# Half of the second modulation's products set between the tiles of two projection groups, and the first modulation's steps in another order

## The chip, the cores and the metric

The kernel runs on one core of one Trainium2 chip. The metric is device time in microseconds (us) of one execution. Three timed runs of the kernel before gave 1221.15, 1223.98 and 1226.54 us; the median is 1223.98. Engines are named as the profile names them: PE is the matrix engine (PEld its weight load), ACT the scalar engine, DVE the vector engine, POOL the general engine, SP the engine that issues nearly all DMAs.

## The reference

One layer of a hybrid model on 512 prompt tokens and 64 sample tokens (8 sequences of 8), width 1024. What matters for this change is the modulation, a product of the conditioning vectors (1 prompt, 8 samples, so 9 rows) with a 1024 x 6144 matrix, and where its six parts are used:

```python
mod = jax.nn.silu(c) @ w_ada + b_ada
sh1, sc1, g1, sh2, sc2, g2 = (m[:, None, :] for m in jnp.split(mod, 6, axis=-1))
h = _rms_norm(x, norm_pre_mix) * (1.0 + sc1) + sh1
mix, ... = _mixer(h, ...)        # h @ w_in (1024 x 3600), retention, GLA, heads, @ w_out
x = x + g1 * _rms_norm(mix, norm_post_mix)
h = _rms_norm(x, norm_pre_ffn) * (1.0 + sc2) + sh2
f = _moe(h, ...)                 # router, 64 experts (8 per token) and a shared one
x = x + g2 * _rms_norm(f, norm_post_ffn)
```

`sh1, sc1` are wanted before the input projection ("first modulation"); `g1, sh2, sc2, g2` only after the mixer ("second modulation").

## The kernel before, in words

Each engine has its own program, written out by hand; the order of the code is the order of execution on that engine, and semaphores tie the engines together. There is no scheduler. Nearly all of SBUF is one array, `arena`, whose parts are used for different things in turn.

The stages, in order of time:

1. Opening (0 to 55 us). Five row tiles of x (four of 128 prompt rows, one of 64 sample rows) are normed and transposed (`x_tile_transposed`, L1796). The first modulation comes in four chunks of 256 columns: `mod1_product(c)` (L1764, weights by the 2 MB DMAs of L534), copied out by ACT (`mod1_rows`, L894), turned into columns by PE (`mod1_columns`, L1772), folded by DVE (`mod1_fold`, L1207 to L1209). Chunk c gives the scale and shift of k tiles 2c and 2c+1 of hT: ACT writes the high part (L902), DVE the exact value and the low part (L1217, L1220) and the sample columns (L1224 to L1227). `project_first(c)` multiplies those two k tiles with projection group 0.
2. Projection (to 226 us). `w_in` has 12 groups of 300 columns. A group's weights come by one 1200 KB DMA (L537) into one buffer, are split by ACT into a high part (L865) and by DVE into a low part (`low_part`, L1231) in one of two buffer pairs, and PE multiplies them with five row tiles (`project`, L1828 prompt, L1821 sample). ACT copies the prompt tiles out of PSUM (L923), DVE the sample tile. SP issues a group's load when the low part of the group before it is done (`s_wlo`). From group 2 on PE runs this as a loop (`pe.Fori`).
3. Retention (to 290 us).
4. GLA (290 to 355 us): a turn for each of five tiles t. In a turn PE makes the scores (L1998), the state product in two halves (L2011), the transposes of the next tile (L1986, `gla_transposed`) and the outputs (L2044, L2046; for the sample tile L2031, L2037). DVE masks the scores (L1437), sums squares (L1387), steps the state (L1451), centres (L1380 to L1382) and finishes the heads of the tile before (`heads`, L1397 to L1403). The second modulation is made here, as 16 pieces (`mod_piece`, L1867): a piece is one k tile of one half (half g=0 is 2048 columns, g1 and sh2; g=1 is sc2 and g2) with a 1 MB weight DMA (L579, four buffers), written as four matmuls, each on 32 columns of the array. After a half's eighth piece four bias products follow (L1872), and DVE folds the half (`mod_fold`, L1266 to L1270). `MOD2_TURNS = (3, 3, 2, 4, 4)` says how many pieces stand in each turn. From the fifth load on, SP issues a piece's load when the piece four before it has been multiplied (`s_ada`).
5. `mixed_transposed` (L1784), the output projection (L2067), the second norm, router, shared expert (to about 520 us).
6. Experts (to 1180 us) and the last sums.

The functions that the change touches and what calls them, with the line numbers of the profile:

## Time and profile before

| | us |
|---|---|
| median of three timed runs | 1223.98 (1221.15 to 1226.54) |
| the profiled execution, its own time | 1225.67 |
| its span in the trace | 1223.5 |
| PE busy in the span | 1106.1 (90%) |
| DVE busy | 903.4 (74%) |
| ACT busy | 642.7 (53%) |
| mean DMA rate | 277 GB/s |

The trace covers 1223.5 of the execution's 1225.67 us. Times in the rows below count from the start of the span. A busy PE is not PE at its peak; the clock that the throttle granted stands in a column of its own (1.00 is full, 0.50 half). What matters is who waits for whom in a stage: an engine that is idle off the chain costs nothing.

### The profile page before, as it was taken

To read this page: it belongs to the slowest core of one execution; us is meant where nothing else is said; L and a number is where in the kernel's file an instruction comes from. 1 tells how busy PE (TensorE), PEld (TensorE's weight loads), DVE (VectorE), ACT (ScalarE), POOL (GpSimd) and SP (SyncE) were. 2 spreads that over 40 slices of the span, in tenths; PEclk is the share of its full clock that TensorE was granted. 3 is DMA by queue.
4 is the path that set the end of the run, shared out by engine and by line. 5 is a ranking of instruction groups with operands and counts; after the bars stand their busy time and mean duration, and the time that the engine had idled before them with its cause. 6 is when DMAs were issued, how large, how long until landed. Compare 5 with 4: busy or idle time off the path is not lost.

```text
span 1223.5 us, 18540 instructions
## 1 busy us (share of the span) xinstructions
PE 1106.1 (90%) x6014; PEld 811.6 (66%) x6014; DVE 903.4 (74%) x1333; ACT 642.7 (53%) x770; POOL 181.9 (15%) x185
## 2 busy tenths in 40 slices
PE   5999999999989999799999999999999999999700
PEld 3899999865444454467777777777777777777500
DVE  4422443365956777579899999989989888888878
ACT  4332221332421233257787777777777777777501
POOL 1000000000110110112222222222222222221102
PEclk9999999998879999899999999999999999999855
DMA  9542221436974143689999999999999999998996
GB/s 341 188 133 80 80 80 40 157 98 202 315 276 132 44 138 120 235 325 381 380 388 391 391 384 385 387 387 381 373 381 383 373 381 379 375 375 314 352 360 210
DMA packets 86545, 339.34 MB, mean 277 GB/s; under 512 B 12561, under 2 KB 36129, under 8 KB 59122
## 3 DMA queue, kind: packets, MB, share of 16 engines
q1 hardware_dynamic: 70130, 301.16, 67.2%
q0 software_dynamic: 16384, 37.78, 8.8%
q8 instruction: 18, 0.29, 0.1%
q14 instruction: 13, 0.11, 0.0%
HBM read 317.00 MB, written 42.86 MB: 294 GB/s over the span
## 4 chain that ended last, share of the span: by engine, by line
PE 46%; DMA 32%; DVE 14%; ACT 6%; issue 2%; SPq 1%; DVEq 0%; POOL 0%; POOLq 0%; ACTq 0%
DMA arena<-in_w_exp_down 28%; PE ps L1828 11%; DVE down_lo L1648 4%; PE ps L2259 4%; PE ps L2067 4%; ACT down_hi L1120 4%; PE ps L2238 3%; PE ps L2239 3%; PE ps L2240 3%; PE ps L1821 2%; PE ps L2242 1%; PE ps L2105 1%; PE ps L2226 1%; DMA arena<-expert_rows 1%; PE ps L2140 1%
## 5 line engine op out<-in xcount | busy, mean ns | idle before, releaser
L1653 DVE TENSOR_TENSOR gu_lo<-w_gu,gu_hi 128x2048 fp32r<-128x2048 f32 (+1 forms) x128 | 258.7, 2022 | 6.4 <-ACT gu_hi L1114 1.1
L1114 ACT ACTIVATE gu_hi<-w_gu 128x2048 fp32r<-128x2048 f32 (+1 forms) x128 | 217.9, 1703 | 0.0
L1648 DVE TENSOR_TENSOR down_lo<-arena,down_hi 128x2048 fp32r<-128x2048 f32 x64 | 146.7, 2293 | 58.0 <-ACT down_hi L1120 58.0
L2238 PE MATMUL ps<-gu_hi,xT_hi 128*112 128x512 f32 x448 | 182.8, 408 | 3.3 <-DVE xT_lo L1658 2.2
L2239 PE MATMUL ps<-gu_lo,xT_hi 128*112 128x512 f32 x448 | 177.9, 397 | 0.0
L2240 PE MATMUL ps<-gu_hi,xT_lo 128*112 128x512 f32 x448 | 177.3, 396 | 0.0
L1120 ACT ACTIVATE down_hi<-arena 128x2048 fp32r<-128x2048 f32 x64 | 122.7, 1918 | 64.0 <-DMA arena<-in_w_exp_down 56.1
L814 POOL DMA_INDIRECT expert_rows<-arena,row_idx x64 | 69.1, 1079 | 356.2 <-ACT arena L1159 340.1
L2259 PE MATMUL ps<-down_hi,actT_hi 128*112 128x512 f32 x256 | 106.6, 416 | 5.5 <-DVE actT_lo L1643 5.5
L807 POOL DMA_INDIRECT arena<-h_rows,token_idx x64 | 80.6, 1259 | 203.1 <-PE ps L2226 156.1
L1828 PE MATMUL ps<-w_hi,hT_hi 128*128 128x300 f32 x352 | 105.6, 300 | 1.4 <-DVE w_lo L1231 1.4
L1828 PE MATMUL ps<-w_lo,hT_hi 128*128 128x300 f32 x352 | 105.7, 300 | 0.0
L1828 PE MATMUL ps<-w_hi,hT_lo 128*128 128x300 f32 x352 | 105.5, 300 | 0.0
L2259 PE MATMUL ps<-down_hi,actT_lo 128*112 128x512 f32 x256 | 101.9, 398 | 0.0
L2259 PE MATMUL ps<-down_lo,actT_hi 128*112 128x512 f32 x256 | 101.6, 397 | 0.0
L2238 PEld LDWEIGHTS ps<-gu_hi,xT_hi 128*112 128x112 f32 x448 | 79.0, 176 | 27.4 <-issue 4.2
L2240 PEld LDWEIGHTS ps<-gu_hi,xT_lo 128*112 128x112 f32 x448 | 78.7, 176 | 26.6
L2239 PEld LDWEIGHTS ps<-gu_lo,xT_hi 128*112 128x112 f32 x448 | 78.8, 176 | 22.0
L2226 PEld LDWEIGHTS ps<-arena 112*128 112x128 f32 x512 | 54.8, 141 | 33.6 <-issue 33.6
L1159 ACT ACTIVATE arena<-ps,slot_w 112x1024 f32<-112x1024 f32 x64 | 71.2, 1113 | 7.1 <-PE ps L2259 7.1
L923 ACT ACTIVATE arena<-ps 128x300 f32 (+1 forms) x48 | 19.7, 421 | 98.4 <-PE ps L1828 96.3
L1237 DVE COPY arena<-ps 64x300 f32<-64x300 f32 (+1 forms) x12 | 5.5, 462 | 89.2 <-PE ps L1821 82.5
(310 smaller groups left out, 1989.8 us busy)
## 6 DMA issues: line engine op xcount, KB each, us to landing
w_gu<-in_w_exp_gate SPq DMA_DIRECT2D x64, 1024.0 KB
w_gu<-in_w_exp_up SPq DMA_DIRECT2D x64, 1024.0 KB
arena<-in_w_exp_down SPq DMA_DIRECT2D x64, 1024.0 KB
arena<-in_w_ada SPq DMA_DIRECT2D x16, 1024.0 KB, 6.9
arena<-in_w_in SPq DMA_DIRECT2D x12, 1200.0 KB, 5.6
arena<-expert_rows SPq DMA_DIRECT2D x9, 1024.0 KB, 13.4
arena<-in_w_ada_first SPq DMA_DIRECT2D x4, 2048.0 KB, 16.2
arena<-expert_rows SPq DMA_DIRECT2D x4, 2048.0 KB, 13.0
```

Source lines behind the costliest of these rows:

```text
L807: g.indirect_dma_start(x_rows[0:T, b % 2], None, h2_rows[:, :], bass.IndirectOffsetOnAxis(token_idx[0:T, b:b + 1].bitcast(U32), 0), bounds ...
L814: g.indirect_dma_start(expert_rows[:, :], bass.IndirectOffsetOnAxis(row_idx[0:T, b:b + 1].bitcast(U32), 0), y_rows[0:T, b % 2], None, boun ...
L1114: a.activation(gu_hi[b % RING][:, :, ks], w_gu[b % U][:, :, ks], ACT.Copy).then_inc(s_ghi, 1)
L1120: a.activation(down_hi[:, :, :], w_dn[b % RING], ACT.Copy).then_inc(s_dhi, 1)
L1159: a.activation(y_rows[0:T, b % 2].rearrange("p (c n) -> p c n", c=2), ps[0:T, 2:4], ACT.Copy, scale=slot_w[0:T, b:b + 1]).then_inc(s_ya, 1)
L1648: v.tensor_tensor(down_lo[:, :, :], w_dn[b % RING], down_hi[:, :, :].bitcast(F32), ALU.subtract).then_inc(s_dlo, 1)
L1653: v.tensor_tensor(gu_lo[b % U][:, :, ks], w_gu[b % U][:, :, ks], gu_hi[b % RING][:, :, ks].bitcast(F32), ALU.subtract).then_inc(s_glo, 1)
L1828: o = pe.matmul(ps[0:ROWS[t], t, 0:GW], x[:, k, cols], w[:, k], start=(k == 0 and n == 0), stop=(k == KT - 1 and n == 2))
L2238: pe.matmul(out, x_hi, gu_hi[r][:, :, k], start=(k == 0), stop=False)
L2239: pe.matmul(out, x_hi, gu_lo[q][:, :, k], start=False, stop=False)
L2240: pe.matmul(out, x_lo, gu_hi[r][:, :, k], start=False, stop=False)
L2259: o = pe.matmul(ps[0:T, 2 + half], x[:, b % 2, k], w[:, k, half * 512:half * 512 + 512], start=(k == 0 and n == 0), stop=(k == FK - 1 and ...
```

## The change: what it does

It has three parts.

First, in the opening PE makes `mod1_product(0)` after three of the five transposed tiles, not after all five; the product of chunk c+1 is put ahead of the two k tiles of chunk c, and its columns between them (`project_first` now takes the k tiles to do). `mod1_product(1)` now stands behind the wait for the low part of w_in's group 0. ACT makes the high part of w_in's group 0 ahead of hT's (and transposed tile 0 ahead of the third square); DVE makes the low part of group 0 between the exact hT and hT's low part. In PE's program ahead of the projection loop (line numbers are each kernel's own: L1796, L1764, L1772, L1807 and L1812 became L1817, L1785, L1793, L1828 and L1833) stood:

```order
L1796 MATMUL ps<-arena 128x128 x32
L1796 MATMUL ps<-arena 128x64 x8
L1764 MATMUL ps<-arena 32x512 x8
L1772 MATMUL ps<-arena 128x9 x4
L1764 MATMUL ps<-arena 32x512 x8
L1772 MATMUL ps<-arena 128x9 x4
L1807 MATMUL ps<-w_hi,hT_hi 128x300
```

and in the changed kernel stand:

```order
L1817 MATMUL ps<-arena 128x128 x24
L1785 MATMUL ps<-arena 32x512 x8
L1817 MATMUL ps<-arena 128x128 x8
L1817 MATMUL ps<-arena 128x64 x8
L1793 MATMUL ps<-arena 128x9 x4
L1785 MATMUL ps<-arena 32x512 x8
L1828 MATMUL ps<-w_hi,hT_hi 128x300
```

The first product moved ahead of the last two transposed tiles, and the second chunk's columns are behind the first k tile of the projection.

Second, the 8 pieces of half g=0 stand in the projection, one behind each prompt tile of groups 3 and 4, with the four bias products behind the last. The 8 pieces of half g=1 stay in the GLA turns, two in each of the four prompt turns. PE's code of groups 2 to 5 is written out; the loop begins at group 6. In PE's program, the piece (L1879, before L1867) inside group 3, where before there was no row between two rows of L1828:

```order
L1849 MATMUL ps<-w_hi,hT_lo 128x300
L1879 MATMUL ps<-arena,condT 9x512 x4
L1849 MATMUL ps<-w_hi,hT_hi 128x300
L1849 MATMUL ps<-w_lo,hT_hi 128x300
L1849 MATMUL ps<-w_hi,hT_lo 128x300
```

The same rows stand between each of the other prompt tiles of groups 3 and 4. In PE's program at the end of the GLA stage, the sample tile's turn (L1867 piece, L1872 bias, L1998 scores, L1784 the first mixed tile's transposes) was:

```order
L1867 MATMUL ps<-arena,condT 9x512 x4
L1998 MATMUL ps<-arena 64x64 x4
L1867 MATMUL ps<-arena,condT 9x512 x12
L1872 MATMUL ps<-arena 9x512 x4
L1784 MATMUL ps<-arena 128x128 x8
```

and is, with the last outputs of the turn ahead (L2064, L2066) and the sample tile's own outputs behind (L2051):

```order
L2064 MATMUL ps<-arena 128x128
L2066 MATMUL ps<-arena 64x128 x2
L2023 MATMUL ps<-arena 64x64 x4
L1805 MATMUL ps<-arena 128x128 x8
L2051 MATMUL ps<-arena 64x128 x4
```

Four pieces and the bias are gone from between the scores (L2023) and the transposes (L1805). The bias is now in the turn before, ahead of that turn's second state half. DVE folds half 0 in projection group 6 and half 1 in GLA turn 3 (before: half 0 in turn 2, half 1 after turn 4).

Third, SP's program. The weights of the early pieces lie in four regions of `proj` that belong to output columns 1552 and up, which group 5 is the first to write. Behind the first two groups' loads (L537, now L550) SP had:

```order
L537 DMA arena<-in_w_in 128x8x300
L556 DMA arena<-in_consts 128x5088
L557 DMA gate_up<-in_gla_gate_up 16x256
L558 DMA gate_bias<-in_gla_gate_bias 128x256
L559 DMA w_router_buf<-in_w_router 128x512
L560 DMA r_bias<-in_router_bias 128x64
L561 UNCONDITIONAL_BRANCH
```

and has:

```order
L550 DMA arena<-in_w_in 128x8x300 x2
L571 DMA arena<-in_consts 128x5088
L572 DMA gate_up<-in_gla_gate_up 16x256
L573 DMA gate_bias<-in_gla_gate_bias 128x256
L574 DMA w_router_buf<-in_w_router 128x512
L575 DMA r_bias<-in_router_bias 128x64
L538 DMA arena<-in_w_ada 128x2048 x2
```

Group 2's load (the second of L550's two) went ahead of the constants. Behind that, where the loop over the groups began at once, SP now has (L538 piece weights, L582 norm rows, L543 bias, L550 the loads of groups 3 and 4):

```order
L582 DMA arena<-in_norm_post_mix 32x512 x2
L582 DMA arena<-in_norm_pre_ffn 32x512 x2
L582 DMA arena<-in_norm_post_ffn 32x512 x2
L543 DMA arena<-in_b_ada 1x512 x4
L550 DMA arena<-in_w_in 128x8x300
L538 DMA arena<-in_w_ada 128x2048 x2
L550 DMA arena<-in_w_in 128x8x300
```

Two piece weights, the norm rows and a half's bias went ahead of group 3's load, two more piece weights ahead of group 4's.

The diff, cut to its core:

```diff
-        w_mod2 = [region(at, 4, 512) for at in (MOD0 + 2 * D, MOD0 + 4 * D, HT0, HT0 + 4 * N)]
-        mod2 = region(MOD0, 2, 512)
-        mod2_bias = region(MOD0 + D, 2, 512)
+        w_mod2_early = [region(PROJ0 + t * IN_W + IN_W - 4 * 512, 4, 512) for t in range(4)]
+        w_mod2 = [region(at, 4, 512) for at in (MOD0 + D, MOD0 + 3 * D, HT0, HT0 + 4 * N)]
+        mod2 = region(MOD0 + 5 * D, 2, 512)
+        mod2_bias = [region(WORK0 + 7200, 512), region(MOD0, 512)]
...
-        MOD2_BANK = 2
-        MOD2_TURNS = (3, 3, 2, 4, 4)
+        MOD2_BANK = (5, 2)
+        MOD2_GROUPS = (3, 4)
...
+            sp.wait_ge(s_wlo, 2)
+            load_win(2)
             sp.dma_start(arena[:, FIRST_W:CONST_W], consts[:, FIRST_W:CONST_W]).then_inc(s_const, 16)
...
-            with sp.Fori(2, NG) as g:
+            sp.wait_ge(s_pj_ev, 2 * PT)
+            sp.wait_ge(s_pjs, 2)
+            load_mod2(0)
+            load_mod2(1)
...
+            load_mod2_bias(0)
+            sp.wait_ge(s_wlo, 3)
+            load_win(3)
+            load_mod2(2)
+            load_mod2(3)
+            sp.wait_ge(s_wlo, 4)
+            load_win(4)
+            for i in range(4, KT):
+                load_mod2(i)
+            with sp.Fori(5, NG) as g:
                 sp.wait_ge(s_wlo, g)
                 load_win(g)
...
             for c in range(NC1):
                 mod1_rows(c)
-                hT_high_part(c)
                 if c == 0:
                     high_part(0, 0)
+                hT_high_part(c)
...
                 mod1_fold(c)
-                hT_low_part(c)
+                hT_whole_part(c)
                 if c == 0:
                     low_part(0, 0)
+                hT_low_part(c)
...
-            for t in range(NT):
+            for t in range(3):
                 x_tile_transposed(t)
             mod1_product(0)
+            for t in range(3, NT):
+                x_tile_transposed(t)
             mod1_columns(0)
-            mod1_product(1)
             pe.wait_ge(s_wlo, 1)
...
+            for c in range(NC1):
+                if c + 1 < NC1:
+                    mod1_product(c + 1)
+                project_first(c, (2 * c,))
+                if c + 1 < NC1:
+                    mod1_columns(c + 1)
+                project_first(c, (2 * c + 1,))
...
+            for g in range(2, 6):
+                pe.wait_ge(s_wlo, g + 1)
+                for t in range(NT):
+                    project(g, g % 2, t)
+                    if g in MOD2_GROUPS and t < PT:
+                        mod_piece()
+            with pe.Fori(3, NG // 2) as i:
...
             for t in range(NT):
                 R = ROWS[t]
-                mod_piece()
+                if t < PT:
+                    mod_piece()
...
                     gla_transposed(t + 1)
-                    for c in range(MOD2_TURNS[t] - 2):
-                        mod_piece()
-                else:
-                    for n in range(MOD2_TURNS[t] - 1):
-                        mod_piece()
                 pe.wait_ge(s_gp, t + 1)
```

## Rows read from the trace of the kernel before

**Rows 1.** Busy time by stretch: us, length, PE, PEld, DVE, ACT, POOL, PEclk, DMA, GB/s

```profile
80.00:120.00 40.00, 40.00 (x293) 40.00 (x292) 10.67 (x9) 10.56 (x15) 0.00 (x0) 1.00 0.29 93
320.00:340.00 20.00, 16.92 (x130) 7.55 (x128) 18.97 (x33) 7.34 (x16) 2.27 (x3) 0.83 0.89 280
```

**Rows 2.** PE in order of time, opening: start us, us, operation [idle before]

```profile
15.53 4.55 PE L1796 MATMUL ps<-arena 128*128 128x128 f32 x24 [2.26 <-DVE arena L1191]
...
20.00 1.92 PE L1764 MATMUL ps<-arena 128*32 128x512 f32 x16
22.65 1.06 PE L1772 MATMUL ps<-arena 128*128 128x9 f32 x8 [0.72 <-ACT arena L894]
...
26.86 3.44 PE L1764 MATMUL ps<-arena 128*32 128x512 f32 x16 [3.15 <-DMA arena<-in_w_ada_first]
31.12 1.03 PE L1772 MATMUL ps<-arena 128*128 128x9 f32 x8 [0.82 <-DVE w_lo L1231]
```

**Rows 3.** L534, the first modulation's weights, and L537 until 75 us

```profile
DMA to landing us min/median/max: 14.2/16.2/20.1
...
DMA to landing us min/median/max: 5.5/10.2/16.1
```

**Rows 4.** Busy time by stretch, opening, columns as in rows 1

```profile
28.00:32.00 4.00, 3.18 (x20) 1.10 (x13) 2.94 (x3) 0.66 (x2) 0.00 (x0) 0.75 1.00 426
```

**Rows 5.** The chain that ended last, 46 to 88 us: start us, us, what

```profile
46.28 1.07 PE ps L1772 x8
...
49.63 1.23 DVE hT_lo L1220
...
55.17 11.68 DMA arena<-in_w_in
...
66.95 2.22 ACT w_hi L865
69.19 2.67 DVE w_lo L1231
...
71.99 13.52 PE ps L1828 x96
85.50 2.20 PE ps L1821 x16
```

**Rows 6.** The page's costliest groups, one of the projection's three prompt products

```profile
L1828 PE MATMUL ps<-w_hi,hT_hi 128*128 128x300 f32 x352 | 105.6, 300 | 1.4 <-DVE w_lo L1231 1.4
```

**Rows 7.** PE in order of time, GLA turns 1 to 3

```profile
308.69 1.05 PE L1867 MATMUL ps<-arena,condT 128*9 128x512 f32 x8
309.67 0.49 PE L2044 MATMUL ps<-arena 128*128 128x128 f32 x2
...
316.05 1.04 PE L1872 MATMUL ps<-arena 1*9 1x512 f32 x8
```

**Rows 8.** PE in order of time, from the sample turn on

```profile
342.21 1.89 PE L1867 MATMUL ps<-arena,condT 128*9 128x512 f32 x8 [5.29 <-DMA arena<-in_w_ada]
...
348.36 1.97 PE L1784 MATMUL ps<-arena 128*128 128x128 f32 x8
...
355.63 7.03 PE L2067 MATMUL ps<-arena 128*128 128x512 f32 x16
```

**Rows 9.** DVE in order of time, GLA

```profile
316.29 0.88 DVE L1437 TENSOR_TENSOR arena<-ps,arena 128x256 f32<-128x256 f32 x2
...
319.74 0.68 DVE L1266 SCALAR_TENSOR_TENSOR arena<-ps,arena 64x512 f32<-64x512 f32 x1
...
327.91 0.88 DVE L1437 TENSOR_TENSOR arena<-ps,arena 128x256 f32<-128x256 f32 x2
...
339.53 0.60 DVE L1437 TENSOR_TENSOR arena<-ps,arena 64x128 f32<-64x128 f32 x2
```

**Rows 10.** Busy time by stretch, GLA, columns as in rows 1

```profile
316.00:320.00 4.00, 3.27 (x33) 1.69 (x29) 3.79 (x9) 0.82 (x2) 1.40 (x2) 1.00 0.98 352
320.00:324.00 4.00, 4.00 (x24) 2.33 (x26) 3.79 (x7) 0.00 (x0) 0.44 (x1) 0.51 0.97 389
```

More of the change, by code:

```diff
@@ L531, in _, with load_mod2, load_mod2_bias @@
             sp.dma_start(arena[:, 0:FIRST_W], consts[:, 0:FIRST_W]).then_inc(s_const, 16)
+            def load_mod2(i):
+                if i >= 4:
+                    sp.wait_ge(s_ada, i - 3)
+                g, k = i // KT, i % KT
+                sp.dma_start((w_mod2_early, w_mod2)[g][i % 4].rearrange("p c n -> p (c n)"),
+                             w_ada[0, k * P:(k + 1) * P, 2 * D + g * 2 * D:4 * D + g * 2 * D]).then_inc(s_wada[i % 4], 16)
+            def load_mod2_bias(g):
+                for c in range(4):
+                    sp.dma_start(mod2_bias[g][c * CG:c * CG + 1], b_ada[0:1, 2 * D:6 * D].rearrange("a (g c n) -> a g c n", g=2, c=4)[:, g, c])\
+                        .then_inc(s_rows, 16)
             def load_mod1(c):
@@ L560, in _ @@
             sp.dma_start(r_bias[:, :], router_bias[0:1, :].broadcast_to([P, E])).then_inc(s_small, 16)
-            with sp.Fori(2, NG) as g:
+            sp.wait_ge(s_pj_ev, 2 * PT)
+            sp.wait_ge(s_pjs, 2)
+            load_mod2(0)
+            load_mod2(1)
+            for g, c, w in ((0, 0, norm_post_mix), (1, 0, norm_pre_ffn), (1, 2, norm_post_ffn)):
+                for half in range(2):
+                    sp.dma_start(mod2[(c + half) * CG:(c + half + 1) * CG, g], w[0:1, half * 512:half * 512 + 512].broadcast_to([CG, 512]))\
+                        .then_inc(s_rows, 16)
+            load_mod2_bias(0)
[8 more added lines that the diff above has]
+            with sp.Fori(5, NG) as g:
                 sp.wait_ge(s_wlo, g)
@@ L615, in _ @@
                 sp.dma_start(head_w[:, n], w.rearrange("a h v -> a (h v)").broadcast_to([P, RET_W])).then_inc(s_small, 16)
-            for i in range(4, 12):
-                load_mod2(i)
             sp.wait_ge(s_st, 16 * 2)
@@ L1218, in hT_low_part @@
                 step(o)
+            def hT_low_part(c):
+                ks = slice(2 * c, 2 * c + 2)
                 v.wait_ge(s_hT, NT + 2 * c + 2)
@@ L1291, in _ @@
                 low_part(g, g % 2)
+                if g == 6:
+                    mod_fold(0)
                 if g - 6 < NT:
@@ L1797, in x_tile_transposed, with project_first @@
                     o.then_inc(s_tr, 1)
-            def project_first(c):
-                for k in (2 * c, 2 * c + 1):
+            def project_first(c, ks):
+                for k in ks:
                     pe.wait_ge(s_hT, NT + 2 * c + 2)
@@ L1849, in _ @@
                 project(1, 1, t)
-            with pe.Fori(1, NG // 2) as i:
-                for b in range(2):
-                    pe.wait_ge(s_wlo, 2 * i + b + 1)
-                    for t in range(NT):
-                        project(2 * i + b, b, t)
             mod_pieces = [0]
```

69 lines of the change are left out of this document (24 added, 45 removed).

## The prediction

> **What bounds the kernel now.** I read the busy time by stretch first. In the projection PE is busy in 40.00 of 40 us at full clock, with the DMAs at 0.29 [rows 1]: what is added to PE there lengthens the run one for one, and there is DMA time to spare. In the GLA turns DVE is busy in 18.97 of 20 us and PE in 16.92 [rows 1]. The chain of waits says what ends last around the two other places: the opening is a ping-pong of PE, ACT and DVE, and before group 2 it passes through a DMA of 11.68 us, that group's weights behind the constants [rows 5]. PE in order of time shows the end of the GLA stage: a piece waits 5.29 us for its weights, and the first mixed tile's transposes come at 348.36 [rows 8], while DVE had begun the last mask of scores at 339.53 [rows 9]. So 8 us of the stage are the pieces and their loads, not GLA.
>
> **Opening.** The first product's weights land at 4.5 + 14.2 = 18.7 us (issue and shortest landing, [rows 3]). The product takes 1.92 [rows 2], to 20.6. Two transposed tiles now come behind it; three took 4.55 us with a wait in it [rows 2], so I put these two (the second is half a tile) at 2.4 and the columns at 23.7, 1.0 later than the 22.65 of before [rows 2]. ACT's high part of w_in takes 2.22, DVE's low part 2.67 [rows 5]. ACT can start at about 23.7, as w_in landed at 5.9 + 16.1 = 22.0 (issue 5.9 us, longest landing, [rows 3]). The low part is then done at about 29.1 instead of 31.0. That looks like a gain of 1.9, but the product of chunk 1, which before ran at 26.86 in the shadow of that wait [rows 2], now starts behind it: 29.1 + 1.92 = 31.0, and before, too, PE went on at 31.12. From there both kernels have the same work up to 36. Further on, the 0.7 us waits for ACT's copy go (twice, 1.4), but the last columns come then at 47.7 instead of 47.35, and from their end to hT's low part are 3.5 us (47.35 to 49.63 + 1.23, [rows 5]): ready at 51.2, where before PE also began its last two k tiles. Order alone: 0.
>
> The clock is what is left. Before, PE was idle 3.15 us ahead of chunk 1's product, the granted clock was 0.75 in the slice behind, and the product took 3.44 instead of 1.92 us [rows 2, 4], which the wait for the low part covered. Now PE is idle for about 4.3 us (24.8 to 29.1) and the slow product is followed by work that PE has waiting. The cover is gone: +1.5, bounds 0 (clock stays) and +2.5 (slow stretch longer).
>
> **Group 2's weights.** PE waited 1.4 us before this group [rows 6]. Its load now goes out at 55.0 and lands 5.5 us later [rows 3]; with 2.2 and 2.7 for the two parts it is ready at 65.6, needed at 70.5. The wait goes: -1.4. Next late is group 3. Ahead of its end stand 1.2 MB (group 2), 3.0 MB (constants and small ones), 2.1 MB (two pieces), 0.4 MB (norm rows) and its own 1.2 MB, 7.9 MB. From 52.1 to 66.9 4.2 MB landed (0.28 MB per us, from [rows 5]); in the opening the rate was 426 GB/s [rows 4]. That gives 73 to 83 us, and 78 to 88 with the two parts, needed at 55.0 + 2 x 15.5 = 86.0 (a group is four times 3.3 + 2.2, 13.52 + 2.20 in [rows 5] with the start). I take no stall; the bound is +2. Pieces 0 to 3 have their weights some 10 us ahead; 4 to 7 are loaded in the 4.3 us steps in which 0 to 3 finish, a group before their use. Group 5's load waits for piece 3, at 103, and is needed at 126.
> The Trainium skill says the same of the order (DMA: Bandwidth & Descriptors, "Queues, rings and completion order": on each DMA engine descriptors are consumed in ring order), so that group 3's weights cannot pass the 2.1 MB of piece weights. By that rule the time is the one worked out above.
>
> **Pieces in the projection.** At full clock a piece takes 0.98 us (308.69 to 309.67), and a half's bias as long (1.04 beside 1.05 in the column of durations) [rows 7]. Nothing lies beside them: 9 x 0.98 = +8.8. The trace has no piece between 300-column matmuls. Lower bound: half of the 1.92 us of the first product, which is the same shape twice, 0.96, so 8.6. Upper bound: a matmul of the projection lasts 300 ns [rows 6] at a step of 141 (13.52 us for 96, [rows 5]); if its tail of 0.16 were not covered at either side of a piece, 8 x 0.32 more, 11.3. I stay at 8.8, the rows in which pieces stand among 128-wide matmuls. The fold of half 0 (1.45 on DVE) is covered in group 6, where DVE has half its time free [rows 1].
> The Trainium skill (TensorEngine Tiling (Array Packing), "Key Properties") says that a change of the tiling mode drains the engine. No run here shows the price in this place. By that rule the upper bound would be the value, and the forecast 1227.0.
>
> **GLA.** Turn 0 loses one piece, 0.98, at full clock: DVE's next mask comes 1.0 earlier. From there DVE sets the pace: 316.29 to 327.91 is a turn of 11.62 with the fold in it (1.45, from 319.74) [rows 9], 10.2 without. The fold leaves turn 2 and the other one enters turn 3, so DVE is 1.0 early at the last mask: 338.5, ended at 339.1. PE has no piece left, and the transposes follow at 339.2 instead of 348.36 [rows 8]: -9.2. Everything behind hangs on them: L2031, L2037, then L2067, which was at 355.63 [rows 8]; DVE's last squares hang on L2037 too, and DVE, done with the heads of tile 3 at 347.6, does not come late to them. The weights of pieces 12 to 15 go out at 294, 298, 304 and 307 and are needed from 312 on. Against the 9.2: in turn 3 DVE needs the state product, and PE has piece and bias (1.95) ahead of its second half, a wait of about 0.3. And PE is idle for about 2 us in each turn now; before, 0.7 us of idle time in 316 to 320 was followed by a clock of 0.51 [rows 10]. One such stretch, half of it off the path, costs 0.5. I take -8.4; bounds -10.2 (also the slow L1784 and L2037 run at full clock) and -4.5 (three slow stretches and their waits).
>
> **Sum.** +1.5 - 1.4 + 8.8 - 8.4 = +0.5 us on the profiled execution's 1225.67, which lies 1.7 above the median of the timed runs. On the median of 1223.98 that is 1224.5. What the GLA stage no longer pays for DMAs, the projection pays in PE time.
>
> **Rivals.**
> 1. The clock falls in the turns (slower). With fewer pieces PE's work in a turn is 7.9 us at full clock (outputs 3.1, two pieces 2.0, state halves 1.2, scores 0.65, transposes 0.8), 14 at half, since a piece at half clock is 1.89 [rows 8] against 1.05. DVE needs 10.2. Each turn at half clock then costs 3.5 us, and the loss decides from two turns on: GLA -1.4, sum +7.5, 1231.5; with three 1235. For it: PE had 0.51 after a stretch 82% busy [rows 10]. Against: most of the stage was at full clock. Chance 0.14.
> 2. Pieces half hidden (faster). If they share fill and drain with the matmuls around them, and cost 4.4 instead of 8.8, with full clock in the opening (0) and GLA at -10.2: 0 - 1.4 + 4.4 - 10.2 = -7.2, 1216.8. For it: PEld, not the stream of columns, is busy throughout [rows 1], and pieces load 9 columns. Against: a piece has 0.98 wherever it stood. Chance 0.15.
> 3. Group 3 late and the drain dear: +0.5 + 2 + 2.5 = +5.0, 1229.0. Chance 0.13. For it the 0.28 MB per us; against, the 434 and more of other stretches.
> 4. The change does not do what it says, as the DMA wait only moves to w_out: its last loads were issued behind the pieces' and L2067 now comes 9 us earlier. Then GLA gives 5 instead of 8.4: +3.9, 1227.9. Chance 0.05. Against: half of the 1 MB loads of this stage are gone.
> Forecast: chance 0.53, own range 1221 to 1228.
>
> **Numbers.** A change of under 0.5% (6.1 us) can't be told from none by a measurement of this kernel. Faster by more: rival 2 and a tail, 0.17. Slower by more: rival 1 and the far end of rival 3, 0.17. Within: 0.66. The range 1218.0 to 1231.0 leaves out most of rivals 1 and 2.
>
> **What would show it.** The profile after should have: PE idle ahead of chunk 1's product and half clock there; no wait before group 2; groups 3 and 4 longer by 4 and 5 us with no idle time; the first mixed tile's transposes at about 348 of the new span (348.4 + 1.5 - 1.4 + 8.8 - 9.2), without a DMA among the releasers of a piece; DVE above 90% in the turns. Wrong would be: a wait for w_in before group 3, a clock near 0.5 through the turns, a piece at 1.2 us or at 0.5 in the projection, or a DMA wait ahead of L2067.

## The result, and the profile after

| | before | after |
|---|---|---|
| median, us | 1224.18 (7 runs, 1221.15 to 1227.60) | 1230.62 (7 runs, 1227.44 to 1235.45) |
| ratio, with its 95% interval | | 1.0059 (1.0035 to 1.0084) |
| profiled execution, its span | 1225.67, 1223.5 | 1230.30, 1228.1 |

The change makes the kernel slower by 0.6%, where the prediction said no change. Twelve more runs of the changed kernel, in a later set, gave 1232.16 and a ratio of 1.0051 (1.0033 to 1.0068). Between the two traces the span grows by 4.6 us. Milestones in both, in us from the start of the span:

| | before | after | step |
|---|---|---|---|
| group 1 starts | 54.99 | 58.31 | +3.3 |
| group 3 starts | 87.54 | 89.64 | -1.2 |
| group 5 starts | 118.38 | 130.96 | +10.5 |
| GLA starts | 290.38 | 301.99 | -1.0 |
| first output projection matmul (L2067, after L2087) | 355.63 | 358.44 | -8.8 |
| end of the span | 1223.5 | 1228.1 | +1.8 |

The opening, PE in order of time in the changed kernel (start us, us, operation, idle time before it and its releaser):

```profile
19.08 3.64 PE L1785 MATMUL ps<-arena 128*32 128x512 f32 x16 [1.71 <-DMA arena<-in_w_ada_first]
...
25.42 1.06 PE L1793 MATMUL ps<-arena 128*128 128x9 f32 x8 [0.71 <-ACT arena L911]
...
30.97 3.21 PE L1785 MATMUL ps<-arena 128*32 128x512 f32 x16 [4.49 <-DVE w_lo L1250]
```

Against [rows 2], the first product takes 3.64 us, not 1.92: it, too, now has a wait ahead of it and runs at half clock, where before it came behind transposed tiles. That is no chance of one execution: over all the traces of this study it took 1.92 to 2.16 us in the nine with the old order and 3.46 to 3.64 in the ten with the new one. So the columns come at 25.42 instead of 22.65, and DVE's low part ends no earlier than before. Then the second slow product follows with nothing to cover it.

The pieces, first PE in order of time, then the chain that ended last, both in group 3 of the changed kernel:

```profile
92.93 0.30 PE L1849 MATMUL ps<-w_hi,hT_lo 128*128 128x300 f32 x1
93.16 1.05 PE L1879 MATMUL ps<-arena,condT 128*9 128x512 f32 x8
94.14 0.41 PE L1849 MATMUL ps<-w_hi,hT_hi 128*128 128x300 f32 x1
94.39 0.30 PE L1849 MATMUL ps<-w_lo,hT_hi 128*128 128x300 f32 x1
```

```profile
68.66 15.91 DMA arena<-in_w_in
...
84.67 2.22 ACT w_hi L882
86.92 2.67 DVE w_lo L1250
89.64 3.60 PE ps L1849 x24
93.23 0.98 PE ps L1879 x8
94.21 3.52 PE ps L1849 x24
...
110.09 3.32 PE ps L1849 x24
```

Two matmuls of the projection start 0.14 us apart. Around a piece the step from 92.93 to 94.14 is 1.21 us and the one behind it 0.25, so a piece costs 1.21 + 0.25 - 2 x 0.14 = 1.18 us, not 0.98. The chain shows the same: the tile behind a piece takes 3.52 where one behind no piece (at 110.09, the first of group 4) takes 3.32. It also shows group 3's load, 15.91 us under way: PE waited only 0.3 us for it.

How much of the 0.2 belongs to the change from the full array to 32 of its columns, other places of the same trace tell. PE in order of time:

```profile
36.00 0.30 PE L1833 MATMUL ps<-w_lo,hT_sample 128*128 128x300 f32 x1
36.13 0.95 PE L1793 MATMUL ps<-arena 128*128 128x9 f32 x8
36.94 0.38 PE L1828 MATMUL ps<-w_hi,hT_hi 128*128 128x300 f32 x1
37.16 0.30 PE L1828 MATMUL ps<-w_lo,hT_hi 128*128 128x300 f32 x1
...
89.64 0.41 PE L1849 MATMUL ps<-w_hi,hT_hi 128*128 128x300 f32 x1 [0.32 <-DVE w_lo L1250]
89.88 0.30 PE L1849 MATMUL ps<-w_lo,hT_hi 128*128 128x300 f32 x1
```

Behind a piece the first step is 0.25 instead of 0.14. Behind a product on the whole array (36.94 to 37.16) it is 0.22, and behind a mere wait (89.64 to 89.88) 0.24: so that half of the 0.2 also stands where the array's division does not change. Ahead of a piece the step is 0.23 (92.93 to 93.16), ahead of the product on the whole array 0.13 (36.00 to 36.13): only this 0.1 goes with the change to 32 columns.

The page's row that answers to [rows 6]:

```profile
L1849 PE MATMUL ps<-w_hi,hT_hi 128*128 128x300 f32 x352 | 106.3, 302 | 0.3 <-DVE w_lo L1250 0.3
```

The end of GLA. PE in order of time in the changed kernel, and DVE's one long wait:

```profile
325.74 0.46 PE L2064 MATMUL ps<-arena 128*128 128x128 f32 x2 [2.37 <-DVE arena L1473]
...
330.04 1.89 PE L1879 MATMUL ps<-arena,condT 128*9 128x512 f32 x8
...
334.07 1.89 PE L1879 MATMUL ps<-arena,condT 128*9 128x512 f32 x8
335.89 1.89 PE L1884 MATMUL ps<-arena 1*9 1x512 f32 x8
337.71 1.12 PE L2036 MATMUL ps<-arena 64*64 64x128 f32 x8
...
350.49 1.97 PE L1805 MATMUL ps<-arena 128*128 128x128 f32 x8 [4.02 <-DVE arena L1459]
```

```profile
338.95 1.25 DVE L1473 SCALAR_TENSOR_TENSOR arena<-arena,ps 128x128 f32<-128x128 f32 x4 [3.60 <-PE ps L2036]
```

No piece waits for a DMA any more (5.29 us in [rows 8]). PE is idle 2.37 us in turn 2, and from 327.2 to 357.9 it has half clock: piece and bias take 1.89 each, and the second state half comes so late that DVE waits 3.60 us. Busy time by stretch (columns as in rows 1), in the changed kernel:

```profile
302.00:322.00 20.00, 19.66 (x180) 10.25 (x182) 14.10 (x29) 9.26 (x18) 1.84 (x2) 1.00 0.98 317
322.00:342.00 20.00, 17.59 (x102) 8.53 (x104) 15.41 (x29) 4.51 (x10) 3.67 (x4) 0.63 0.22 89
342.00:358.40 16.40, 11.65 (x112) 8.89 (x111) 13.51 (x22) 5.58 (x14) 1.83 (x2) 0.52 0.43 152
```

and in the kernel before, over its whole GLA stage:

```profile
290.40:310.00 19.60, 19.60 (x140) 9.49 (x140) 8.89 (x21) 6.21 (x11) 1.59 (x2) 0.76 0.95 318
310.00:330.00 20.00, 19.27 (x155) 9.36 (x157) 19.01 (x32) 7.66 (x16) 2.09 (x3) 0.83 0.88 316
330.00:355.60 25.60, 19.62 (x176) 9.36 (x169) 17.02 (x29) 5.33 (x13) 3.67 (x4) 0.73 0.79 262
```

Both have about 30 us at half clock in this stage (2 x (1 - PEclk) x length, summed). In the kernel before it lay in three stretches (turn 0, turn 2, and the last turn behind the wait for weights); now it is one. The first piece of turn 0 shows it, in the kernel before and in the changed one:

```profile
291.82 1.90 PE L1867 MATMUL ps<-arena,condT 128*9 128x512 f32 x8
```

```profile
302.76 1.05 PE L1879 MATMUL ps<-arena,condT 128*9 128x512 f32 x8
```

That the kernel before had so much of it in this one execution is what the experiments turned out to hinge on.

### The profile page after: what moved, and what is told of

It is laid out like the page before. It is cut to its first block, busy times and chain, and to the rows that moved or that the text cites. A ratio compares the mean times of both kernels' runs of the same rounds, so it can differ in the third digit from the quotient of the medians.

```text
span 1228.1 us, 18511 instructions
## 1 busy us (share of the span) xinstructions
PE 1106.4 (90%) x6014; PEld 810.5 (66%) x6014; DVE 903.5 (74%) x1333; ACT 641.8 (52%) x770; POOL 187.2 (15%) x185
## 4 chain that ended last, share of the span: by engine, by line
PE 46%; DMA 30%; DVE 15%; ACT 6%; issue 1%; SPq 0%; DVEq 0%; POOL 0%; POOLq 0%; ACTq 0%
DMA arena<-in_w_exp_down 26%; PE ps L1849 10%; PE ps L2279 5%; PE ps L2087 4%; DVE down_lo L1669 4%; ACT down_hi L1137 3%; PE ps L2258 3%; PE ps L2259 3%; PE ps L2260 3%; DMA arena<-in_w_in 2%; PE ps L1842 2%; PE ps L2262 2%; PE ps L2246 1%; PE ps L2125 1%; DMA arena<-in_w_ada_first 1%
## 5 line engine op out<-in xcount | busy, mean ns | idle before, releaser
L831 POOL DMA_INDIRECT expert_rows<-arena,row_idx x64 | 71.9, 1123 | 350.6 <-ACT arena L1176 333.3
L2246 PEld LDWEIGHTS ps<-arena 112*128 112x128 f32 x512 | 54.8, 141 | 33.6 <-issue 33.6
L1849 PEld LDWEIGHTS ps<-w_hi,hT_hi 128*128 128x128 f32 x352 | 66.2, 188 | 5.7 <-ACT arena L940 3.4
```

The source lines that it names most:

```text
L831: g.indirect_dma_start(expert_rows[:, :], bass.IndirectOffsetOnAxis(row_idx[0:T, b:b + 1].bitcast(U32), 0), y_rows[0:T, b % 2], None, boun ...
L1849: o = pe.matmul(ps[0:ROWS[t], t, 0:GW], x[:, k, cols], w[:, k], start=(k == 0 and n == 0), stop=(k == KT - 1 and n == 2))
```

## The experiments

Seventeen runs in five sets, of fifteen new kernels, the changed kernel once more (after_again) and one kernel twice (win2_early_again); within a set all ran on the same chip beside the kernel before, whose median was 1223.95 to 1226.42. "Groups 3+4" is the time from the start of group 3 to that of group 5. "GLA" is from its first transposes to the first matmul of the output projection, behind it the us at half clock in that stretch. These and the span are of the profiled execution.

| kernel | median (runs) | ratio to before, interval | group 1 | groups 3+4 | GLA (half clock) | span |
|---|---|---|---|---|---|---|
| before | | | 55.0 | 30.8 | 65.2 (30) | 1223.5 |
| changed | 1230.62 (7) | 1.0059, 1.0035-1.0084 | 58.3 | 41.3 | 56.5 (31) | 1228.1 |
| after_again | 1232.16 (12) | 1.0051, 1.0033-1.0068 | 59.3 | 41.3 | 59.3 (38) | 1233.1 |
| old_opening | 1228.48 (12) | 1.0040, 1.0017-1.0064 | 55.7 | 41.3 | 56.5 (31) | 1225.4 |
| new_opening_alone | 1226.15 (12) | 1.0009, 0.9984-1.0033 | 59.7 | 30.8 | 65.2 (30) | 1230.6 |
| product_ahead_of_wait | 1233.98 (6) | 1.0080, 1.0052-1.0108 | 55.7 | 41.3 | 56.5 (31) | 1226.3 |
| fill_before_product | 1229.60 (12) | 1.0048, 1.0025-1.0072 | 56.7 | 41.3 | 56.5 (31) | 1227.6 |
| pieces_in_fours | 1231.35 (12) | 1.0058, 1.0031-1.0084 | 58.5 | 39.5 | 60.5 (40) | 1233.5 |
| narrow_pieces | 1225.83 (10) | 1.0011, 0.9985-1.0036 | 58.6 | 35.7 | 56.5 (31) | 1221.4 |
| last_piece_out_of_half | 1232.58 (8) | 1.0064, 1.0038-1.0089 | 55.9 | 41.3 | 57.0 (27) | 1229.1 |
| combined | 1230.72 (12) | 1.0041, 1.0018-1.0063 | 54.1 | 39.5 | 60.0 (38) | 1231.9 |
| fill_turns | 1226.06 (12) | 1.0005, 0.9983-1.0026 | 59.2 | 41.3 | 50.9 (3) | 1220.1 |
| fill_turns_old_opening | 1226.10 (12) | 0.9999, 0.9980-1.0018 | 57.5 | 41.3 | 50.9 (3) | 1220.6 |
| before_fill | 1223.66 (12) | 1.0013, 0.9989-1.0037 | 54.1 | 30.8 | 55.7 (0) | 1218.3 |
| fill_fours_product | 1220.31 (12) | 0.9980, 0.9955-1.0005 | 57.4 | 39.5 | 50.9 (3) | 1218.4 |
| fill_fours_old_opening | 1223.20 (12) | 0.9982, 0.9962-1.0003 | 59.0 | 39.5 | 52.3 (7) | 1225.3 |
| win2_early | 1220.25 (7) | 0.9941, 0.9916-0.9966 | 56.0 | 30.8 | 60.5 (14) | 1218.2 |
| win2_early_again | 1222.07 (12) | 0.9997, 0.9970-1.0024 | 55.9 | 30.8 | 54.0 (10) | 1213.2 |
| win2_early_fill | 1219.70 (12) | 0.9980, 0.9957-1.0004 | 57.3 | 30.8 | 56.4 (0) | 1217.1 |

### The opening

old_opening gives the changed kernel the opening of before; new_opening_alone gives the kernel before the new one. In PE's program the two differ by this, from the new to the old (the steps of the chunks behind it, and ACT's and DVE's order, go with it):

```diff
-            for t in range(3):
+            for t in range(NT):
                 x_tile_transposed(t)
             mod1_product(0)
-            for t in range(3, NT):
-                x_tile_transposed(t)
             mod1_columns(0)
+            mod1_product(1)
             pe.wait_ge(s_wlo, 1)
```

> The changed kernel with the opening of before (PE's, ACT's and DVE's order), all else as changed. Theory A, the opening costs 3.3 us because chunk 0's and chunk 1's products now run at half clock on the path: PE's group 1 starts at about 55.0 instead of 58.3 in the trace, group 3 no longer than before + 0 to 2, and the time is 3.3 us below the changed kernel, some 2 to 3 above before. Rival B, the clock in the opening is chance, or a late weight load gives the time back: within 1 us of the changed kernel, 6 above before.

> The kernel before with the new opening alone. Theory A: group 1 starts at about 58.3 instead of 55.0, both first products take over 3 us, time 2.5 to 3.5 above before. Rival B: group 1 at 55 to 56.5 and the time within 1 us of before; then the delay in the changed kernel comes from something else in it.

In the traces the new opening costs 2.6 us (58.3 against 55.7) in the changed kernel and 4.7 us (59.7 against 55.0) in the kernel before. In time it is 1.1 us on the kernel before (1.0009), and 1.3 to 2.3 on the changed one (1.0051 and 1.0059 less 1.0040). The interval of the first contains 1 and those of the others overlap, so the times alone don't show a cost. The next two take one cause each.

```diff
+            mod1_product(1)
             pe.wait_ge(s_wlo, 1)
             for c in range(NC1):
-                if c + 1 < NC1:
+                if 0 < c < NC1 - 1:
                     mod1_product(c + 1)
```

> The changed kernel, but chunk 1's product stands ahead of PE's wait for the low part of group 0 of w_in, as it did before the change. Theory A (the opening loses 3.3 us because slow products are no longer covered by that wait): the product starts at about 26.9, takes 3.4 at half clock in the shadow of the wait, PE begins the first k tile at about 31.1 instead of 34.1, and group 1 starts at 55.3 to 56.3 instead of 58.3; time 2 to 3 us below the changed kernel's. Rival (the loss comes from the new order of ACT and DVE, exact hT and low parts, which hangs on chunk 0's columns and not on chunk 1's product): group 1 stays at 58 or moves by under 0.7.

```diff
             mod1_columns(0)
+            for n in range(4):
+                pe.matmul(ps[:, 4, 0:FIRST_W], ident, arena[:, 0:FIRST_W], start=True, stop=True)
             pe.wait_ge(s_wlo, 1)
```

> The changed kernel with four more matmuls of 320 columns on PE between chunk 0's columns and the wait for the low part of group 0; they write a bank that nobody reads, and only take up idle time. Theory A (idle time ahead of the product is what lets the clock fall): granted clock 1.00 behind 27, chunk 1's product at about 1.9 instead of 3.2 us, group 1 at about 57.0 instead of 58.3. Rival (the clock fell for what PE did before 25, when the first product already ran at half clock): product still 3.2 or more and group 1 at 58.3 or later.

PE in order of time with the product ahead of the wait:

```profile
26.44 3.46 PE L1785 MATMUL ps<-arena 128*32 128x512 f32 x16 [0.65 <-DMA arena<-in_w_ada_first]
31.50 0.38 PE L1828 MATMUL ps<-w_hi,hT_hi 128*128 128x300 f32 x1 [1.61 <-DVE hT_lo L1239]
```

and with the fillers:

```profile
26.04 4.07 PE L1860 MATMUL ps<-arena 128*128 128x320 f32 x8
30.68 1.92 PE L1785 MATMUL ps<-arena 128*32 128x512 f32 x16 [0.57 <-DVE w_lo L1250]
```

In the trace both go Theory A's way: with the slow product in the shadow of the wait group 1 comes at 55.7, and with PE kept busy through the wait the product takes 1.92 us and group 1 comes at 56.7. ACT and DVE kept their new order in both, so the slow product on PE's path is what costs. What Theory A says of the clock did not hold. Busy time with the fillers (columns as in rows 1):

```profile
26.00:30.00 4.00, 4.00 (x10) 2.42 (x9) 3.57 (x6) 2.55 (x3) 0.00 (x0) 0.57 1.01 434
```

The clock fell all the same, and the fillers themselves ran at half clock, from 26.0 to 29.4. Here and with the product ahead (from 26.2) PE had not been idle for more than 0.71 us at a time since the first product, so the clock does not fall for the 4.49 us behind it: in this the rival is right, and what it does fall for is open. What differs is when it comes back: at 29.4 with the fillers, at 29.6 with the product ahead, at 33.6 in the changed kernel, where it had fallen at 26.8 and PE then stood idle.

The size is less sure, as the start of group 1 differs from one execution to the next. In the nine traces with the old opening it lies between 54.1 and 59.0 (mean 56.0), in the seven with the new one between 55.9 and 59.7 (mean 58.5), and in the second kernel with the product ahead of the wait, fill_fours_product, at 57.4. Counted from the start of the first product it takes 39.2 to 40.5 us in those seven, 37.4 and 38.9 with the product ahead, 37.6 with the fillers. So the new opening costs some 2.5 us, and 3.3 was this pair of executions. The times do not follow: 1.0080 from six runs, with the lowest of them the profiled one, is no gain. Why those executions were slower is not settled; an effect of 2 us is at the edge of what 12 runs tell, and the traces carry this point alone.

### The pieces in the projection

```diff
                     project(g, g % 2, t)
-                    if g in MOD2_GROUPS and t < PT:
-                        mod_piece()
+                    if g in MOD2_GROUPS and t == PT - 1:
+                        for n in range(4):
+                            mod_piece()
```

> The changed kernel with the early pieces behind the last prompt tile of groups 3 and 4, four at a time, instead of one behind each prompt tile. Groups 3 and 4 took 10.65 us longer than before in the trace, 1.18 for each piece and the bias, where a piece itself took 0.98. Theory C, each change between a piece and a projection tile costs 0.1 to 0.2 beside the piece: with 2 in place of 8 stretches the two groups are 9.2 to 9.5 longer than before, time 1.2 below the changed kernel. Rival D, the extra 0.2 belongs to each piece (its weights' or its columns' fetch beside the running DMAs): groups still 10.6 longer, no change in time. Should the piece weights come late when four stand together, PE would wait for a DMA ahead of a piece, and the time would rise.

```diff
-                    o = pe.matmul(ps[c * CG:c * CG + NCOND, MOD2_BANK[g]], condT[:, k, :], (w_mod2_early, w_mod2)[g][i % 4][:, c], start=(k == 0), stop=False)
+                    n = 16 if g == 0 and k else 512
+                    o = pe.matmul(ps[c * CG:c * CG + NCOND, MOD2_BANK[g], 0:n], condT[:, k, :], (w_mod2_early, w_mod2)[g][i % 4][:, c, 0:n], start=(k == 0), stop=False)
```

> The changed kernel with seven of the eight early pieces cut from 512 to 16 columns (their part of the modulation is left out, so the outputs differ). Loads, waits and the changes between pieces and tiles stay. Theory C: a narrow piece costs its switch, 0.2 to 0.4, so groups 3 and 4 together are 10.65 - 7 x 0.8 = 5.0 longer than before, of it 1.9 piece 0 and bias, 0.4 for each narrow piece. Rival D: the narrow piece costs nearly nothing (below 0.15), 3 us in all.

PE in order of time, pieces in fours, then a narrow piece:

```profile
102.88 3.62 PE L1879 MATMUL ps<-arena,condT 128*9 128x512 f32 x32
```

```profile
97.80 0.30 PE L1849 MATMUL ps<-w_hi,hT_lo 128*128 128x300 f32 x1
98.03 0.23 PE L1880 MATMUL ps<-arena,condT 128*9 128x16 f32 x8
98.19 0.41 PE L1849 MATMUL ps<-w_hi,hT_hi 128*128 128x300 f32 x1
98.43 0.30 PE L1849 MATMUL ps<-w_lo,hT_hi 128*128 128x300 f32 x1
```

Four pieces in a row take 3.62 us, 0.9 each. Groups 3 and 4 are 1.8 us shorter with two breaks instead of eight, 0.3 us for each break saved. A piece with 16 of its 512 columns still costs 0.39 + 0.24 - 2 x 0.14 = 0.35 us. So of the 10.5 us that the pieces add (10.48 by the starts of groups 3 and 5, where the expectations say 10.65), some 8 are columns and 2 to 2.5 are the breaks. Narrow pieces gave back 5.6 us of the trace of these groups and 5 to 6 us of the time (1.0011 against 1.0051 and 1.0059). The fours gave back nothing in time. In the profiled execution GLA took 60.5 us with 40 at half clock, but that was the slowest of the twelve (1235.8 us), and their mean granted clock, 0.945, is that of after_again; why the other eleven show no gain is open.

### The clock in the turns

```diff
                             o.then_inc(s_rowtile, 1)
-                            mod_piece()
+                            if t < PT - 1:
+                                mod_piece()
...
                     gla_transposed(t + 1)
+                    if t == 1:
+                        mod_piece()
```

> The changed kernel with GLA's pieces as 2, 3, 2, 1 over the prompt turns: in turn 3 the only piece and its bias stand ahead of the scores, and nothing stands between the two halves of the state product. Theory D (in turn 3, at half clock, piece and bias of 3.8 us between the halves hold DVE's step of the state back by 3.6 us): that wait shrinks to under 1.5, and the first mixed tile's transposes come 1.5 to 3 us earlier than in the changed kernel, counted from the start of GLA (48.5 there, so 45.5 to 47). Rival (PE's whole work of the turn at half clock is the bound, so its order does not matter): 48 to 49 as there, and the time is the changed kernel's.

> The changed kernel with three edits at once: the opening of the kernel before, the early pieces four together behind the last prompt tile of groups 3 and 4, and the last piece out of the state halves as in last_piece_out_of_half. By the three traces the parts give -2.6, -1.8 and (Theory D) about -2, so 6 us below the changed kernel: 1224 to 1225, level with the kernel before. Rival (parts of the traces are given back by the clock further on, as the time of the kernel with pieces in fours did not fall with its trace): only the opening's part is seen, 1227 to 1229.

The wait of 3.60 us in turn 3 went, but the piece that was moved up came before its weights, in PE's order of time:

```profile
322.24 1.90 PE L1879 MATMUL ps<-arena,condT 128*9 128x512 f32 x8 [1.66 <-DMA arena<-in_w_ada]
327.46 1.90 PE L1879 MATMUL ps<-arena,condT 128*9 128x512 f32 x8 [1.11 <-DMA arena<-in_w_ada]
```

DVE then waited 2.97 us at 330.5. The transposes came 49.4 us into the stage against 48.5: Theory D got turn 3's wait right and the gain wrong, and the rival's number nearly held. combined, built on the same step, had 38 us of half clock in GLA and gained nothing. Both failures pointed away from the order and to the clock.

```diff
+            FILL = (15, 15, 28)
             gla_transposed(0)
             for t in range(NT):
...
                     gla_transposed(t + 1)
+                if t >= 2:
+                    for n in range(FILL[t - 2]):
+                        pe.transpose(ps[:, 3, 384:512], ident, ident)
                 pe.wait_ge(s_gp, t + 1)
```

> The changed kernel with transposes of the identity added on PE where it only waits for DVE in the last three GLA turns: 15 in turn 2, 15 in turn 3, 28 in turn 4 (0.14 us each at full clock, so 2.1, 2.1 and 3.9 us). They write columns that nobody reads. Theory E (PE's idle time in the turns, new because the pieces are gone, is what the clock falls after; the slow turn 3 then costs 3.6 us of waiting on DVE and slow transposes and sample outputs behind it): the clock stays at 1.00 from 327 on, the wait of 3.60 us shrinks to under 0.5, the first mixed tile's transposes come 48.5 - 3.3 = 45.2 us after the start of GLA, the stage takes 50 to 52 instead of 56.4 us, and the time falls by 4 to 6 us. Rival (the clock falls whatever PE does with that time, as a power limit would make it): same half-clock stretch of about 30 us, slower fillers then hold PE back, stage 56 to 58.

> The changed kernel once more, beside the others on one chip, for its time with more runs and for a second trace. Theory E expects the half clock of the GLA turns again (about 30 us of it behind the idle time in turn 2), a DVE wait of 3 to 4 us in turn 3, a time of 1230 to 1232 and a mean granted clock below that of the kernel before; the rival (the half clock of turn 3 was chance of one execution) expects turns at full clock in about half the cases.

> fill_turns with the opening of the kernel before. Theory A and E together: 2.5 us (opening) and 4 to 6 us (clock in the turns) below the changed kernel, 1223 to 1225, level with the kernel before or just under it. Rival (clock lost again elsewhere): 1227 to 1229, as with the old opening alone.

The whole GLA stage by busy time, changed kernel once more, then fill_turns:

```profile
303.40:362.80 59.40, 51.85 (x391) 29.32 (x392) 43.36 (x78) 19.65 (x42) 7.36 (x8) 0.68 0.54 180
```

```profile
302.70:353.50 50.80, 45.70 (x448) 29.16 (x449) 41.30 (x74) 18.97 (x40) 7.34 (x8) 0.97 0.63 208
```

and PE in order of time in fill_turns:

```profile
323.88 1.80 PE L2043 MATMUL ps<-arena 128*128 128x128 f32 x15
326.42 0.46 PE L2068 MATMUL ps<-arena 128*128 128x128 f32 x2 [0.73 <-DVE arena L1473]
...
332.77 1.04 PE L1884 MATMUL ps<-arena 1*9 1x512 f32 x8
...
347.40 1.09 PE L1805 MATMUL ps<-arena 128*128 128x128 f32 x8 [3.31 <-DVE arena L1459]
...
353.53 7.03 PE L2091 MATMUL ps<-arena 128*128 128x512 f32 x16
```

Useless transposes of 1.8, 1.9 and 3.3 us hold the clock at full but for 3 us: bias at 1.04 instead of 1.89, no wait on DVE's side, the stage 50.9 us instead of 56.5 and 59.3. The time falls by 6.1 us against the changed kernel in the same set, and the loss against the kernel before is gone. This is the clearest verdict of the study. With the old opening on top nothing more came in time.

The kernel before got the same treatment, 15 such transposes at the end of turn 3 and 30 ahead of the last turn's third piece:

> The kernel before with transposes of the identity where PE only waits in GLA: 15 at the end of turn 3, 30 in the last turn ahead of the third piece, whose weights PE awaits for 5.3 us there. They write columns that nobody reads. If the clock can be held here as well: pieces, bias, transposes and sample outputs behind the wait at full clock, the output projection 3 to 4 us earlier, time 2 to 4 us below the kernel before; then the change itself, with the clock held in both, costs 2 to 4 us, which is the opening. If the clock falls anyway: same time as before.

```profile
289.80:345.50 55.70, 51.51 (x508) 27.56 (x509) 44.93 (x79) 19.02 (x40) 7.34 (x8) 1.00 0.95 341
```

```profile
336.45 1.04 PE L1867 MATMUL ps<-arena,condT 128*9 128x512 f32 x8 [0.65 <-DMA arena<-in_w_ada]
338.95 1.04 PE L1867 MATMUL ps<-arena,condT 128*9 128x512 f32 x8 [1.46 <-DMA arena<-in_w_ada]
```

With full clock throughout the old GLA stage takes 55.7 us, not 65.2. With the clock held in both, taking eight pieces out of it is worth 4.9 us (55.74 less 50.87), half of what the profiled execution had promised. In time, though, the fillers gave the kernel before nothing. Two things bear on it. The same GLA code without a filler took 54.0 us in win2_early_again, with only 10 us at half clock, so other executions lose less than the profiled one. And at full clock the last pieces wait for their weights (0.65 and 1.46 us above), so the loads set the end of the stage. Whether that is all is not shown.

### Group 2's load, and what beats what

```diff
             sp.wait_ge(s_hTl, NT + 2 * NC1)
+            sp.wait_ge(s_wlo, 2)
+            load_win(2)
...
-            with sp.Fori(2, NG) as g:
+            with sp.Fori(3, NG) as g:
```

> The kernel before with one edit: group 2's load of w_in goes out ahead of the constants. Expected by the prediction's term: PE's wait of 1.4 us before group 2 goes, group 2 starts at 70.5 instead of 72.0, group 3 without a wait of over 0.3; time 0 to 2 us below the kernel before. Rival (group 3 becomes late as its load now stands behind the constants): a wait of 1 us or more at group 3 and no gain.

> win2_early once more. If the load of group 2 alone gives its 1.4 us and the rest of the 4.7 was the clock of those executions, the median comes to 1222 to 1224 now; if the gain is all its own, 1219 to 1221 again.

> win2_early with the fillers of before_fill. If both gains are real they add up: 2 to 4 us below win2_early. If the clock falls anyway: the time of win2_early.

The projection from group 1 on takes 169.8 us instead of 171.5: the wait is gone, as forecast, and group 3 does not wait. The first set gave 0.9941 (7 runs), the second 0.9997 (12 runs), and their intervals do not overlap; so the traces show the 1.4 to 1.7 us, and what they are worth in time is not settled. win2_early_fill came out at 0.9980 with 1 just inside its interval.

> fill_turns with two more edits: the early pieces four together behind the last prompt tile of groups 3 and 4, and chunk 1's product ahead of the wait for the low part of w_in. Theory (both costs are work on PE's path and add up once the clock is held): -1.8 and -2.4 us against fill_turns in the trace, groups 3 and 4 at 39.5 instead of 41.3, 1221.5 to 1223.5. Rival (the clock falls in turn 0, as it did with the pieces in fours): a half-clock stretch of 10 us near 300 and the time of fill_turns, 1226.

> The changed kernel with the opening of the kernel before, the early pieces four together, and the fillers in the last three GLA turns. By the traces 1.2 us below fill_fours_product (group 1 is 39.3 us behind the first transposes instead of 40.5): 1218.5 to 1221, the kernel before at 1224, ratio 0.995 to 0.998. Rival (the half clock comes back in the opening or in turn 0): 1222 to 1225, no gain.

With the clock held, the fours and the covered product do add up: 3.1 us below fill_turns by the ratios, where the traces' terms gave 4.2. So the changed kernel's own idea, mended in three places, comes to 0.9980 (0.9955 to 1.0005). The old opening did no better there (0.9982): in its trace the first product came late, at 20.92, and group 1 at 59.0. No version beats the kernel before beyond its interval in every set; the one-line load of group 2 comes nearest for its size.

## Why the prediction was wrong, point by point

**The opening: +1.5 forecast, +3.3 measured.** The failed step is "The product takes 1.92": the trace of before had shown that product behind 4.55 us of transposes, and it was moved to behind a wait (1.71 us). It ran at half clock, 3.64 us, and everything that hangs on it, the columns and DVE's low part, stood where it had stood, not 1.9 us earlier. The cost of the second slow product was forecast rightly in kind and size (3.21 against 1.92), with its idle time (4.3 forecast, 4.49 measured), though the fillers' trace has the clock fall without that idle time. 58.3 less 55.0 is both together and, by the spread over the traces, some 0.8 us of chance: the means differ by 2.5, the forecast's upper bound.

**Group 2's weights: -1.4, measured -1.2** with the 0.3 us wait at group 3. Right, cause and size. (60.5 + 2.2 + 2.7 is 65.4, not 65.6, which changes nothing.)

**Pieces in the projection: +8.8 forecast, +10.5 measured,** inside the bounds of 8.6 and 11.3. The forecast took a piece to stretch nothing around it. The failed step is "Nothing lies beside them": a piece stretches the step ahead of it and the start of the next tile, 1.18 us a piece. The Trainium skill (TensorEngine Tiling (Array Packing), "Key Properties") has the rule, that changing the tiling mode drains the engine; by it the forecast had put 11.3. The trace agrees in kind at most: of the 0.2 us beside each of the eight pieces, half stands also behind a wait or a product on the whole array, where the mode does not change, and no run parts the other half from other causes.

**GLA: -8.4 forecast, -8.8 in the two traces, but for another reason.** The number agrees by luck. The forecast had DVE set the pace with a wait of 0.3 us in turn 3; it was 3.60, at half clock. This is rival 1 for one turn: it priced a turn at half clock at 3.5 us, and the transposes came 3.8 us later into the stage than in fill_turns (48.5 against 44.7). From turn 3's mask of scores (L1459 there and here) to the transposes the forecast's terms give 13.7 us; fill_turns took 13.7 and the changed kernel 17.3.

What made up for it is turn 0. The step "Turn 0 loses one piece, 0.98, at full clock" had it wrong: in the trace of before turn 0 ran at half clock. Turn 2's mask came 25.9 us into the stage there, 21.7 in before_fill and both traces of win2_early, where turn 0 had full clock, and 20.8 in the changed kernel. So 0.9 us was the piece and 4.2 the clock, which the forecast did not count and no run ties to the change: with its code turn 0 was slow in part in after_again (22.4) and pieces_in_fours (24.8).

The deeper failure is that the -9.2 was taken from one execution of before in which the stage had 30 us at half clock. Four traces of that GLA code without fillers have 65.2, 65.2, 60.5 and 54.0 us, a mean of 61.2; the seven with the changed kernel's GLA code have 56.5 to 60.5, a mean of 57.4. The difference is 3.8 us, and 4.9 with the clock held. That is the term that was mis-sized: 8.4 instead of 4 to 5.

**The sum.** With the opening at its mean, +2.5 - 1.2 + 10.5 - 4.5 = +7.3. The 1.0 us by which retention differs between the two traces is left out: it had half clock at 238 in the trace of before and none in that of after, and other traces of both kernels show either. Measured are 6.4 (7 runs) and, by the ratio of the second set, 6.2. The forecast's range reached to 1231.0 and holds the median; a loss that can be measured had been given a chance of 0.17.

**The rivals.** Pieces half hidden is refuted by the 1.18 us. Group 3 late was 0.3 us, not 2; the stretch around the pieces was real but took 1.7 of its 2.5. The wait that moves to w_out was under 0.2 us here (the first output projection took 7.20 us, 7.03 before); in win2_early_again, with the shortest old GLA stage, PE waited 1.9 us for w_out, so part of what that stage gave was lost again there. (By its own terms rival 1's PE work is 7.75 us, not 7.9.)

**What behaved as the profile said it would:** no DMA wait ahead of a piece or of L2067's successor, 0.3 us before group 3, DVE busy 93% of turns 1 and 2 (19.35 of the 20.75 us between masks), the transposes at 350.5 where about 348 was forecast.

**Still open.** Why turn 0 and the last turns of the same code have full clock in one execution and half in the next was not tried. And the 1.8 us behind the output projection in the changed kernel's trace: 1.0 of it lies in the experts' stream, from the first split of a down matrix to the last (624.0 us against 623.0). That takes 622.1 to 625.5 us over all traces with no order by kernel, so I take it for chance; the other 0.8 is not placed.

## What to carry to other kernels

Before a stage's time is taken as what a change can win, ask at what clock that one execution ran it; the same code took 54 to 65 us here. Moving work off a matrix engine that waits for another engine does not free its time only: it leaves idle time, and here a dense stretch behind it ran at half clock, so a piece of work may be worth its place as a filler. Work that is slow for such a reason belongs in the shadow of a wait, and single small matmuls of another shape are better put together than spread.

## What the runs showed of the hardware

The mean granted clock and the time go together over executions of one and the same kernel. In the 142 executions of the kernel before in the five sets, the clock went from 0.944 to 0.957 and the time from 1214.3 to 1232.0 us, with a correlation of -0.81: at 0.945 and below the mean time was 1229.5 (6 executions), at 0.956 and above 1218.6 (13). The Trainium skill (TensorE: Matmul & The Clock Gate, "A second HAM failure mode: psum-queue depth-cycling") says that an engine which idles briefly but often between groups of matmuls oscillates between its two rates; it tells it of a kernel that cycles through PSUM banks. The trace of before agrees in kind: its GLA stage had 0.50 from 289.4 to 299.6, from 320.1 to 326.9 and from 340.6 to 354.2, and 1.00 between, and ahead of the second of these PE had been idle 0.73 us. The changed kernel's trace has one stretch of 30.7 us.

What PE does in its idle time in the GLA turns need not be useful to keep the clock: 7.0 us of transposes of the identity over three turns (1.8, 1.9 and 3.3), put where it waited, were enough to leave 3 us of half clock in the stage, and saved 6.1 us in 1232. In the kernel before, with the same treatment and no half clock left in the stage, the time did not fall.
